# Cached keys turned by DMA ahead of the attention instead of by TensorE inside it, in a one-core hybrid decoder layer

## The reference

```python
for window, dil in ((128, 1), (512, 4), (2048, 16)):
    idx = wb + arange(T) - dil * arange(129)          # wb = 2048 cached rows, T = 4
    s = einsum("bthd,btjhd->bthj", q, k[:, idx]) / 8  # then softmax, then the same rows of v
```

## Time and profile before

| | |
|---|---|
| median of three runs | 1765.56 us |
| span of the profiled execution | 1761.8 us |
| TensorE busy | 1712.2 us (97%) |
| VectorE busy | 1127.0 us (64%) |
| ScalarE busy | 876.3 us (50%) |
| GpSimd busy | 2.2 us |
| moved by DMA | 233.74 MB, mean 133 GB/s |

### The profile page before, as it was taken

The page is one execution under the profiler, slowest core; times in us unless marked ns, Lnnn a source line. Parts: engine busy times, 40 slices in busy tenths (PEclk is TensorE's granted clock), DMA queues, the critical chain, the costliest instruction groups (busy, mean ns, idle before and its releaser), DMA issues.

```text
span 1761.8 us, 30467 instructions
## 1 busy us (share of the span) xinstructions
PE 1712.2 (97%) x12158; PEld 1595.8 (91%) x12158; DVE 1127.0 (64%) x2077; ACT 876.3 (50%) x1645; POOL 2.2 (0%) x12
## 2 busy tenths in 40 slices
PE   7999999999999999999998999999999999999998
PEld 7999999756668999888778899999999999999998
DVE  5499998686675677345467667644576533676633
ACT  7322223655667676555455455534545533555433
POOL 0000000000000000000000000000000000000000
PEclk9999999999999999999999999999999999999999
DMA  8233221365315645443533334444445444444443
GB/s 247 64 119 114 84 86 37 132 225 192 127 43 154 185 144 156 149 131 108 164 120 96 118 114 140 133 136 138 133 143 155 139 140 139 132 144 147 144 136 100
DMA packets 349219, 233.74 MB, mean 133 GB/s; under 512 B 7979, under 2 KB 322465, under 8 KB 349071
## 3 DMA queue, kind: packets, MB, share of 16 engines
q1 hardware_dynamic: 344232, 222.96, 41.4%
q10 hardware_dynamic: 4847, 8.83, 1.4%
HBM read 220.68 MB, written 11.50 MB: 132 GB/s over the span
## 4 chain that ended last, share of the span: by engine, by line
PE 85%; DVE 7%; ACT 4%; issue 3%; SPq 1%; DMA 0%; ACTq 0%; DVEq 0%
PE bank L1240 79%; PE bank L1237 6%; ACT whi L621 1%; SPq L458 1%; DVE cv L1841 1%; DVE wlo L1854 1%; DMA raw<-in_w_mk_dram 0%; DVE Y L1841 0%; DVE Pp L1845 0%; DVE RSCF L1977 0%; DVE Pp L2130 0%; ACT wide L635 0%; DVE op_lo L1841 0%; DVE XT L2232 0%; DVE C L1981 0%
## 5 line engine op out<-in xcount | busy, mean ns | idle before, releaser
L1240 PE MATMUL bank<-op_hi,whi 128*128 128x352 f32 x1632 | 539.5, 331 | 4.9 <-DVE wlo L1854 2.6
L1854 DVE TENSOR_TENSOR wlo<-raw,whi 128x1024 fp32r<-128x1024 f32 (+1 forms) x312 | 373.8, 1200 | 246.0 <-ACT whi L621 245.7
L1240 PE MATMUL bank<-op_hi,wlo 128*128 128x352 f32 x1632 | 525.4, 322 | 0.0
L1240 PE MATMUL bank<-op_lo,whi 128*128 128x352 f32 x1632 | 524.5, 321 | 0.0
L621 ACT ACTIVATE whi<-raw 128x1024 fp32r<-128x1024 f32 (+1 forms) x312 | 325.1, 1043 | 287.7 <-PE bank L1240 94.5
L1240 PEld LDWEIGHTS bank<-op_hi,whi 128*128 128x128 f32 x1632 | 307.5, 188 | 14.6 <-issue 9.9
L1240 PEld LDWEIGHTS bank<-op_lo,whi 128*128 128x128 f32 x1632 | 308.4, 189 | 0.6
L1240 PEld LDWEIGHTS bank<-op_hi,wlo 128*128 128x128 f32 x1632 | 307.3, 188 | 0.0
L1240 PE MATMUL bank<-fhi,whi 128*128 128x352 f32 x528 | 171.2, 324 | 0.0
L1240 PE MATMUL bank<-fhi,wlo 128*128 128x352 f32 x528 | 170.7, 323 | 0.0
L1240 PE MATMUL bank<-h1hi,whi 128*128 128x352 f32 x480 | 158.0, 329 | 0.0
(11 more groups left out here) (287 smaller groups left out, 2299.7 us busy)
## 6 DMA issues: line engine op xcount, KB each, us to landing
raw<-in_w_up_dram SPq DMA_DIRECT2D x132, 512.0 KB, 3.7
raw<-in_w_down_dram SPq DMA_DIRECT2D x48, 512.0 KB, 3.7
raw<-in_w_out_dram SPq DMA_DIRECT2D x24, 512.0 KB, 3.8
raw<-in_w_xq_dram SPq DMA_DIRECT2D x24, 512.0 KB, 3.8
raw<-in_w_xo_dram SPq DMA_DIRECT2D x24, 512.0 KB, 3.8
raw<-in_w_in_dram SPq DMA_DIRECT2D x20, 512.0 KB, 3.8
raw<-in_w_down_dram SPq DMA_DIRECT2D x24, 384.0 KB, 3.3
cached<-in_cache_win_k_dram SPq DMA_DIRECT2D x8, 1024.0 KB, 5.9
```

What stands on the lines that cost most here:

```text
L1240: return pe.matmul(out, lhsT, rhs, start=first, stop=last, skip_group_check=shared)
L1854: dve.tensor_tensor(wlo[v % SLOTS][:, 0:nk, :], raw[v % SLOTS][:, 0:nk, :], whi[v % SLOTS][:, 0:nk, :].bitcast(F32), ALU.subtract).then_in ...
```

## The change

The 896 cached key rows of each of the 8 samples are turned by DMA. A piece is 128 of the 512 key columns of one sample, so there are 32 pieces. The pieces run as a pipeline of three on SP's queue, behind the weights of units 8 to 35 (one piece behind each, two behind units 24, 27, 30 and 33):

- `gather_old` copies the 384 old rows of a sample into a dense scratch tensor `keys_old`.
- `turn_keys(p)` starts two DMA transposes, which work on 2-byte elements: the 512 near rows and the 384 old ones, into `HALVES`.
- `part_keys(p-1)` waits for the transposes of piece p-1 and for the join of piece p-2, and moves low and high halves with four SBUF-to-SBUF transfers into `PLANES`.
- `join_keys` on GpSimd interleaves them into 4-byte words with two copies into `WORDS`, after the piece before has been stored.
- `keep_keys(p-2)` stores `WORDS` to the scratch tensor `keys_turned`.

In the attention `window(n)` for keys is then one transfer of the same 1.835 MB from `keys_turned`. `key_turn` and the copies to `KTS` are gone; `key_scores` runs once per sample, in its last slot (r = 6, 13, 20, 27), with 8 matmuls. Window 0 is no longer loaded inside the input stage, since its place holds the new tiles. `product` always uses bank 4.

```diff
+    PIECES = AT * BD
+    PIECES_AT = {u: 1 for u in range(NT, 3 * NT)}
+    PIECES_AT.update({u: 2 if u % 3 == 0 else 1 for u in range(3 * NT, XFIRST)})
...
+            if kind == "k":
+                sp.wait_ge(*at("kept", AT * b + AT - 1))
+                load(cached_t[n % len(cached)][:, :, :], A["keys_turned"][b], name, (n, OLD // P - 1))
+                return
...
+        def gather_old(b):
+            if b >= 2:
+                sp.wait_ge(*at(f"gathered{b % 2}", b - 2))
+            rows = A["cache_win_k"][0, b].rearrange("s h d -> s (h d)").rearrange("(g r) n -> g r n", r=16)
+            load(A["keys_old"][b].rearrange("(g r) n -> g r n", r=4), rows[0:OLD // 4, 0:4, :], f"gathered{b % 2}", b)
+
+        def turn_keys(p):
+            b, k = divmod(p, AT)
+            if p >= 2:
+                sp.wait_ge(*at("planes", (p - 2, 1, 1)))
+            if k == 0:
+                sp.wait_ge(*at(f"gathered{b % 2}", b))
...
+            sp.dma_start_transpose(t[:, :, OLD:KEYS], near).then_inc(*mark(name, (p, "near"), 16))
+            sp.dma_start_transpose(t[:, :, 0:OLD], A["keys_old"][b].bitcast(U16)[:, cols]).then_inc(*mark(name, (p, "old"), 16))
+
+        def part_keys(p):
+            sp.wait_ge(*at(f"turned{p % 2}", (p, "old")))
+            if p >= 1:
+                sp.wait_ge(*at("joined", (p - 1, 1)))
+            for e in range(2):
+                for h in range(2):
+                    sp.dma_start(PLANES[DH * e:DH * e + DH, h, :], HALVES[p % 2][h:P:2, e, :]).then_inc(*mark("planes", (p, e, h), 16))
+
+        def keep_keys(p):
+            b, k = divmod(p, AT)
+            sp.wait_ge(*at("joined", (p, 1)))
+            sp.dma_start(A["keys_turned"][b, :, k, :], WORDS[:, :]).then_inc(*mark("kept", p, 16))
...
+        p = 0
         for u in range(SLOTS, XFIRST + SLOTS - 1):
             weight(u)
+            if SLOTS <= u < SLOTS + BD:
+                gather_old(u - SLOTS)
+            for _ in range(PIECES_AT.get(u, 0)):
+                key_stream(p)
+                p += 1
...
-            if u == 3 * NT:
-                window(0)
...
         sp.wait_ge(*at("unit", LAST_IN))
+        window(0)
+        sp.wait_ge(*at("kept", PIECES - 1))
         window(1)
...
+        def join_keys(p):
+            pool.wait_ge(*at("planes", (p, 1, 1)))
+            if p:
+                pool.wait_ge(*at("kept", p - 1))
+            words = WORDS[:, :].bitcast(U16).rearrange("p (n h) -> p h n", h=2)
+            for h in range(2):
+                pool.tensor_copy(words[:, h, :], PLANES[:, h, :]).then_inc(*mark("joined", (p, h)))
...
-        def key_turn(n):
...
+        def key_scores(b):
+            g, i = divmod(b, 4)
+            n = ORDER_W.index(("k", b))
+            c = n % len(cached)
+            pe.wait_ge(*at(f"cached{c}", (n, OLD // P - 1)))
+            for c0, c1, bk in ((0, 512, 6), (512, KEYS, 7)):
+                for k in range(AT):
+                    ins = mm(bank[bk][32 * k:32 * k + 32, 0:c1 - c0], QW[:, g, P * i + 32 * k:P * i + 32 * k + 32], cached_t[c][:, k, c0:c1], i == 0 and bk == 6, i == 3, True)
```

More of the change, by code:

```diff
@@ L208, in layout @@
     stage_f = mn("stage_f", 146656, [P, 3, P])
-    cached = [mn(f"cached{i}", o, [P, KTILES, AW]) for i, o in enumerate((160064, 47104, 119808))]
+    PLACES = (47104, 160064, 119808)
+    cached = [mn(f"cached{i}", o, [P, KTILES, AW]) for i, o in enumerate(PLACES)]
+    cached_t = [mn(f"cached_t{i}", o, [P, AT, KEYS]) for i, o in enumerate(PLACES)]
+    HALVES = [mn(f"HALVES{i}", 160064 + 3584 * i, [P, 2, KEYS], U16) for i in range(2)]
+    PLANES = mn("PLANES", 160064 + 7168, [P, 2, KEYS], U16)
+    WORDS = mn("WORDS", 160064 + 10752, [P, KEYS])
     ATT = mn("ATT", 20480, [P, AT, NTOK])
@@ L214, in layout @@
     PT = mn("PT", 38912, [P, 2, SEQ])
-    KTS = [mn(f"KTS{i}", 16384 + 2048 * i, [P, AT, P]) for i in range(2)]
     QW = mn("QW", 61440, [P, 2, 544])
@@ L363, in window_of, with batch_slot @@
         return n, n % len(cached)
[L365 to L369, removed]
+    PIECES = AT * BD
+    PIECES_AT = {u: 1 for u in range(NT, 3 * NT)}
+    PIECES_AT.update({u: 2 if u % 3 == 0 else 1 for u in range(3 * NT, XFIRST)})
+    def batch_slot(r):
+        return r // KTILES if 0 <= r < GROUP and r % KTILES == KTILES - 1 else -1
     QTS = [[(0, P), (P, P), (2 * P, (CW if c < CH - 1 else SP0) - 2 * P)] for c in range(CH)]
@@ L504, in _ @@
                 load(ws[:, :], A["sample_bias"], "tables", "s")
+        for p in range(p, PIECES + 2):
+            key_stream(p)
         sp.wait_ge(*at("unit", LAST_IN))
+        window(0)
+        sp.wait_ge(*at("kept", PIECES - 1))
         window(1)
@@ L605, in _ @@
         pool.memset(U[:, :, 0:PAD], 0.0).then_inc(*mark("pads", 0))
+        def join_keys(p):
[5 more added lines that the diff above has]
+                pool.tensor_copy(words[:, h, :], PLANES[:, h, :]).then_inc(*mark("joined", (p, h)))
+        for p in range(PIECES):
+            join_keys(p)
         pool.wait_ge(*at("unit", LAST_IN))
@@ L794, in sample @@
         def sample(g, r):
[L796 to L799, removed]
-                    act.wait_ge(*at("ssc", n - 2))
-                act.activation(KTS[n % 2][:, :, :], bank[4 + n % 2][:, :].rearrange("p (k n) -> p k n", k=AT), ACT.Copy).then_inc(*mark("ktsa", n))
             if r == GROUP + 2:
@@ L1417, in product @@
             i, hp = STEPS[s]
-            take(product_bank(s), "att", s)
+            take(4, "att", s)
             for e in range(2):
@@ L2064, in sample @@
         def sample(g, r):
-            if 0 <= r < GROUP and not on_scalar(g * GROUP + r):
-                n = g * GROUP + r
-                dve.wait_ge(*at("ktr", n))
-                if n >= 2:
-                    dve.wait_ge(*at("ssc", n - 2))
-                dve.tensor_copy(KTS[n % 2][:, :, :], bank[4 + n % 2][:, :].rearrange("p (k n) -> p k n", k=AT)).then_inc(*mark("ktsd", n))
             if r == GROUP + 1:
-                dve.wait_ge(*at("ssc", (g + 1) * GROUP - 1))
+                dve.wait_ge(*at("ssc", 4 * g + 3))
                 if g:
@@ L2134, in attended @@
             dve.wait_ge(*at("pv", s))
-            dve.tensor_copy(ATT[:, hp, i * P:(i + 1) * P], bank[product_bank(s)][:, 0:P]).then_inc(*mark("att", s))
+            dve.tensor_copy(ATT[:, hp, i * P:(i + 1) * P], bank[4][:, 0:P]).then_inc(*mark("att", s))
         def mix_low(c, m):
```

44 lines of the change are left out of this document (20 added, 24 removed).

## The result

The change makes the kernel slower: 1803.89 us, the median of four runs (1800.81 to 1805.59), against 1764.46 us of before (1758.58 to 1768.46, four runs) on the same chip. The ratio is 1.0225, with a 95% interval of 1.0203 to 1.0248. The forecast was 1779 us; the result lies inside the range, but the kernel lost 39.4 us and not 13.4.

A forecast was written before the change was run, and what follows sets the result against it. The prediction took TensorE as the bound, with VectorE also full in the input stage. Span 1761.8 - 33 (attention) + 46 (copies) = 1774.8 us, plus 3.8 around it, gave 1779 us, range 1730 to 1830.

The forecast's parts named there:

- What bounds the kernel: Whole kernel: TensorE busy 97% of the span; in the input stage TensorE and VectorE both full, the convolution finishing just in time.
- The attention's gain, 33 us: Attention: turns and copies to KTS go, scores get cheaper; 17 + 16 = 33 us gained, between 20 and 40.
- the turns' 33 us: Attention: removing the key turns of 56 key tiles, 0.59 us each, takes 33.0 us off TensorE.
- group 1: Attention's second group of samples (410 to 480 us): TensorE stays the bound; gain 15 to 19, taken as 17 us.
- group 0: Attention's first group of samples (335 to 380 us): window data, with window 3 landing about 362, limits the gain to 16 us.
- The copies take VectorE's time whole, 46 us: Input stage: GpSimd's join copies, 1.0 us each, block VectorE for their whole length; 46 us lost, between 35 and 65.
- taps above 1284: Input stage: VectorE's taps averaging above 1284 ns would be a sign for the forecast that copies cost VectorE time.
- The loop, 7.5 us with "every SP wait counts": Input stage, between pieces: issue 3.0, landing 2.5, copies 2.0 us; just fits the 7.4 and 8.3 us available per piece.
- Traffic "cost at nothing": Input stage: 57 MB added, some 225 GB/s beside 94, against 325 GB/s seen; weights have cover, so no cost.
- Rival 2, the key stream too slow: Input stage: late SP steps hold weights once a piece exceeds 7.9 us plus 15/32; 1818 us at 11 us a piece; chance 0.18.
- Rival 1, the copies free: Input stage: copies cost VectorE nothing, only the loop counts, losing 0 to 10 us; 1733 to 1743 us; chance 0.30.
- Rival 3: Attention: windows or the softmax chain bound it, so 20 us gained in place of 33; no chance given.

The follow-up runs named there:

- e8: Changed kernel with only samples 4 to 7 turned by DMA (16 pieces, 12.5 us apart) and window 0 loaded in the input stage: 1764.90 us, ratio 1.0008.
- e4: Changed kernel without the key stream; key windows load other cached rows of the same size: 1734.90 us, ratio 0.9838.
- e3: Changed kernel with each joining copy replaced by two clears of WORDS, so GpSimd reads nothing: 1804.69 us, ratio 1.0233.
- e1: Changed kernel with the two joining copies of each piece cut to 16 of 896 elements: 1777.34 us, ratio 1.0073.
- e12: e1 with a third HALVES tile for pieces 0 to 23, so transposes wait for the parts of piece p-3: 1773.94 us, ratio 1.0067.
- e5: e1 with parts cut to 32 of 896 columns, the store to 16 of 896 words, and key windows loading other rows: 1747.63 us, ratio 0.9912.
- e13: e1 with the two DMA transposes of a piece replaced by two plain loads of the same size: 1752.62 us, ratio 0.994.
- e7: Changed kernel with a piece's steps on SP reordered: store first, then parts, then transposes: 1794.61 us, ratio 1.0182.
- e14: e10 with pieces spread to unit 31, none behind the weights of units 16 and 17, and window 0 behind unit 34: 1749.67 us, ratio 0.9923.
- e11: Changed kernel, all 32 pieces, with the join on ScalarE, store first, pieces spread evenly over units 8 to 35: 1899.13 us, ratio 1.0778.
- e10: e8 with the join as one ScalarE copy per piece, its last store one unit and window 0 two units later: 1756.70 us, ratio 0.9972.

## Why the prediction was wrong

The attention gained 28.4 us where 33 were forecast, so the error lies in the input stage: it lost 68.9 us, where the prediction had 46, and for another reason. That the time lies inside the stated range is luck. The working also counts the gathers twice: 57 MB of added traffic, where the profile shows 50.3 more (284.02 - 233.74).

- **What bounds the kernel: right.** TensorE and VectorE were both full in the input stage, and e8 shows how little slack there was: 18 us of longer taps moved the sums by 12.5 us.
- **The attention's gain, 33 us: right in kind, a little large.** e4 has 29.2, the changed kernel 28.4. The scores cost 1.7 us a sample, in place of 1.9 (or 2.0 as taken in the sum), so the turns' 33 us were taken off as forecast. Both groups fell a little short: when group 1 begins, the prompt's scores are 13 us ahead of before (16 forecast), and it adds 15 (17 forecast). In group 0 window 3 waited at 434, some 30 us into the attention, where the prediction had its data at 27, and TensorE was busy only 35.3 of the first 45 us at a clock of 0.85.
- **The copies take VectorE's time whole, 46 us: this is the step that failed.** The taps did grow, by 178.4 - 154.1 = 24.3 us, and that cost nothing (e3 has the same time without it), since VectorE was no longer full: it waited for weights. The mark "taps above 1284" came true for a mechanism that wasn't the cause; VectorE's sums began late, at 363.58, and TensorE waited for them only 4.5 us. The contention itself is much as the prediction took it. In e8, where VectorE is full, its taps (first three rows) and GpSimd's two copies of one piece (last two) take turns:

```profile
112.37 1.28 DVE L1937 SCALAR_TENSOR_TENSOR C<-U,cw,C 128x1024 f32<-128x1024 f32 x1
113.69 2.05 DVE L1937 SCALAR_TENSOR_TENSOR C<-U,cw,C 128x1024 f32<-128x1024 f32 x1
115.78 2.05 DVE L1937 SCALAR_TENSOR_TENSOR C<-U,cw,C 128x1024 f32<-128x1024 f32 x1
...
112.92 1.81 POOL L686 COPY WORDS<-PLANES 128x896 uint16<-128x896 uint16 x1 [6.89 <-DMA keys_turned<-WORDS]
114.63 2.18 POOL L686 COPY WORDS<-PLANES 128x896 uint16<-128x896 uint16 x1
```

  The copy that starts inside the first tap leaves that tap at 1.28 us and ends 1.1 us after it (114.73); the second tap, already begun, ends 1.0 us after the copy (115.74); the second copy ends 1.1 us after that, and the third tap 1.0 us after the second copy. So each copy costs VectorE 2.05 - 1.28 = 0.77 us, where the prediction took 1.0, and a copy that takes 1.20 us alone takes up to 2.2. The clears of e3 left the taps at 1284 ns. By the rule of the Trainium skill (SBUF — State Buffer, Who interferes with whom), reading GpSimd instructions contend and block for the whole instruction: the traces agree with both halves. What failed is the cost put on it, in a stage where VectorE waited for weights.
- **The loop, 7.5 us with "every SP wait counts": the mechanism was right, and sized too small.** It took 10.3 to 10.85 us. Of the missing 2.75 in the turn shown above, the copies are 1.6, the parts' issue 0.9, the landing 0.25. Here the contention does count, on GpSimd's side: a pair takes 2.33 us alone and 3.6 beside VectorE, inside the loop. With the copies cut short it still took 9.85 us (e1), and with one wait less 9.70 (e12).
- **Traffic "cost at nothing": the second step that failed.** The estimate compared bytes (225 + 94 GB/s) with 325 GB/s seen once, as if all bytes cost the engines the same. Before, 108 GB/s took a share of 0.34 from 90 to 150 us; e5 takes 0.46 more for 61 GB/s more (nearly all transposes), which is 133 GB/s for a whole share, against 318 before. (e5 also cuts its parts into packets under 512 B, so this alone would overstate the transposes' load.) e1 and e13 give the same by another way: 139 GB/s more for 0.67 and 173 more for 0.58 are 207 and 298 GB/s for a whole share, and if a third of e1's bytes are transposed, those alone run at 128. So a transposed byte holds the engines some 2.4 times as long, an estimate from these shares. They were full at 247 GB/s (e1), and e12 shows that a wait removed there comes back as issue time.
- **Rival 2, the key stream too slow: this is what came,** at 0.18. Its threshold (7.9 us plus 15/32) was passed, and its formula gives 347 - 252 - 15 = 80 us for 10.85 us a piece, against 69 measured. It also named the case that copies wait for VectorE, with 9 to 10 us a piece, and the rows of e8 above show them doing so. Its marks were all seen: `whi` waiting for `raw`, over 8 us between stores. The latency that stood for its transposes' price was no threat: by the Trainium skill (VectorE: DVE Perf Modes, The three transpose paths) one block takes 1309 ns, and as forecast that is no rate: the 14 blocks of a piece would take 18.3 us, and a piece went by every 10.85 us, its two transposes landing 4.1 and 3.4 us (medians) after their issue.
- **Rival 1, the copies free:** the copies' load on VectorE cost next to nothing, as it said, but not for its reason (the taps did grow), and its time, 1733 to 1743, did not come, since it took the loop at 7.5 us. **Rival 3** fell: 28 us arrived.

What stays open: how e13's 25 us divide between the DMA engines and SP's issue; what the 18 us left with plain loads and a short join are; how much of the join's 27 us comes from the contention's lengthening of the copies (107.2 us in all, where 32 pairs alone would take 75), since no run has the same join without it; and why the loop of e7 shrank by 0.3 us and not 0.6 (the copies grew from 1719 to 1777 ns in the mean, 0.12 us a piece, which explains only a part).

## What to carry to other kernels

Work taken off a full engine by DMA has to be priced as a loop: issue, landing and each engine's step, in the order of the queue that also carries the weights. Compare that loop with the period that the stage leaves. Above it nearly every excess microsecond is paid by all engines (e3 against e1: 1.0 us a piece, 27 us in 32 pieces), and a contention matters by what it adds to the loop. When it doesn't fit, halve the amount before giving the idea up: 16 pieces 12.5 us apart, joined on an engine that VectorE doesn't contend with, kept half of the gain (e14, 0.9923). And an in-order engine with time to spare is no place for a step if what stands before it there waits for the queue that waits for the step (e11 against e10).

## What the runs showed of the hardware

- Two DMA transposes of a piece (512 and 384 rows by 256 columns of 2 bytes) issue in 1.26 and 1.28 us (medians), twice a plain transfer's 0.60, and load the DMA engines some 2.4 times as much per byte as weights (the estimate above). The changed kernel moves 69675 packets under 512 B, e13, with plain loads in their place, 11307: the transposed 14.7 MB go in some 58000 packets of about 250 B. Whether that is why they load the engines more, no run shows.
- A GpSimd copy of 896 2-byte elements took 1.20 us alone and up to 2.2 beside a full VectorE (median 2.03 in e8), whose tap behind it took 2.05 us in place of 1.28: each waits for the other's instruction to end. Clears cost VectorE nothing (e3). A ScalarE copy of twice that took 2.2 us and left VectorE's taps untouched (e10).
- With full DMA engines and nothing else to wait for (e12) the issue of a transpose on SP stretched from 1.25 to 2.3 us, up to 4.1.
- The granted clock of TensorE fell with its waits: 0.73 between 250 and 270 us of the changed kernel, where it was busy 12.45 of 20 us, against 1.00 and 19.44 before. The sample's scores took 3.17 us at 0.53, nearly all at the lower level of 1.2 GHz, after a stretch (404 to 411 us) in which TensorE was busy 3.85 of 7 us, and 1.71 us at 1.00. So part of what a late weight costs comes after it has landed: the 1440 products with `h1hi` and `h1lo` were busy 479.8 us in place of 466.3.
